# All pairs of four more feed-forwards as halved products, and a fifth ring place that is lent to them

## The reference

```
lat = lat + 0.5 * ml[2] * _swiglu(_modulate(lat, norm_ffn1_g[l], ml[0], ml[1]), *ffn1)
cx  = cx  + 0.5 * mc[2] * _swiglu(_modulate(cx, ...), *ffn1)
h_cx = _modulate(cx, norm_mix_g[l], mc[3], mc[4])
out_cx, s_f, s_b = _token_mixer(h_cx, *mix_w, zero_state, zero_state)    # holds the scan
out_lat, _, _ = _token_mixer(_modulate(lat, ...), *mix_w, s_f, s_b)
lat = lat + 0.5 * ml[8] * _swiglu(_modulate(lat, norm_ffn2_g[l], ...), *ffn2)
def _swiglu(h, w1, w3, w2):  return (jax.nn.silu(h @ w1) * (h @ w3)) @ w2
```

## Time and profile before

| | |
|---|---|
| median of the timed runs | 3034.98 us |
| the profiled execution's own time | 3039.78 us |
| its span, first to last instruction | 3038.0 us |
| PE busy | 2864.5 us, 94% |
| DVE, ACT, POOL busy | 987.1, 550.3, 318.5 us |
| granted PE clock, mean | 0.971 |
| the chain that ended last | PE 85%, DMA 13%, all else 1% or less |

### The profile page before, as it was taken

One profiled execution on the slowest core, in us unless ns is written; L12 is line 12 of the kernel. 1 busy time (PEld: TensorE's weight loads), 2 busy tenths in 40 slices (PEclk: granted clock), 3 DMA queues, 4 the chain that ended last, 5 costly groups with the idle time before them and its releaser, 6 DMA issues.

```text
span 3038.0 us, 38593 instructions
## 1 busy us (share of the span) xinstructions
PE 2864.5 (94%) x16882; PEld 2420.1 (80%) x16882; DVE 987.1 (32%) x1846; ACT 550.3 (18%) x822; POOL 318.5 (10%) x344
## 2 busy tenths in 40 slices
PE   8999999999999999999999999999999999866666
PEld 6888888888888788889888888889988888533432
DVE  3764034331433315333014433523146412210111
ACT  2101222123211101010023206210012340200000
POOL 0000011100121000058001210028100000000000
PEclk9999999999999999999999999999999999988887
DMA  9774443344334566464444344364433228899998
GB/s 402 270 273 171 153 146 133 128 144 153 138 138 131 202 235 230 173 236 166 154 153 153 135 142 153 127 234 168 153 126 136 99 104 339 368 430 430 430 432 361
DMA packets 74139, 641.40 MB, mean 211 GB/s; under 512 B 8304, under 2 KB 9584, under 8 KB 21232
## 3 DMA queue, kind: packets, MB, share of 16 engines
q1 hardware_dynamic: 71376, 631.55, 54.9%
q10 hardware_dynamic: 2592, 7.33, 0.6%
HBM read 637.80 MB, written 1.05 MB: 210 GB/s over the span
## 4 chain that ended last, share of the span: by engine, by line
PE 85%; DMA 13%; DVE 1%; issue 0%; ACT 0%; SPq 0%; DVEq 0%; ACTq 0%
PE ps L1236 34%; PE ps L1258 18%; DMA ring<-in_w_moe 12%; PE ps L1214 8%; PE ps L1433 7%; PE ps L1246 3%; PE ps L1269 3%; PE ps L1463 2%; PE ps L1034 2%; PE ps L1322 1%; DMA ring<-in_w_ada 1%; PE ps L1440 1%; PE ps L1056 1%; PE ps L1161 1%; PE ps L1408 0%; PE ps L1411 0%
## 5 line engine op out<-in xcount | busy, mean ns | idle before, releaser
L1236 PE MATMUL ps<-ring 128*128 128x256 f32 x2560 | 560.7, 380 | 0.1
L1236 PEld LDWEIGHTS ps<-ring 128*128 128x128 f32 x2560 | 485.5, 191 | 67.8 <-issue 1.9
L1258 PE MATMUL ps<-work,ring 128*128 128x256 f32 x2464 | 537.8, 380 | 0.0
L1258 PEld LDWEIGHTS ps<-work,ring 128*128 128x128 f32 x2464 | 466.5, 190 | 64.0 <-issue 2.1
L1236 PE MATMUL ps<-h,ring 128*128 128x256 f32 x2240 | 497.3, 384 | 5.0 <-DVE rs L1898 2.2
L1236 PEld LDWEIGHTS ps<-h,ring 128*128 128x128 f32 x2240 | 429.3, 193 | 68.3 <-issue 6.6
L1895 DVE TENSOR_TENSOR work<-work,ps 128x512 f32<-128x512 f32 (+4 forms) x286 | 133.7, 467 | 631.1 <-PE ps L1236 389.4
L2612 POOL TENSOR_TENSOR work<-work 128x128 f32<-128x128 f32 x168 | 100.1, 632 | 1194.7 <-ACT work L1676 1194.7
L1433 PE MATMUL ps<-h,ring 128*128 128x256 f32 x928 | 205.0, 379 | 0.5 <-DVE h L1901 0.5
L1433 PEld LDWEIGHTS ps<-h,ring 128*128 128x128 f32 x928 | 174.9, 190 | 27.4 <-issue 4.2
L1895 DVE TENSOR_TENSOR work<-work 128x128 f32<-128x128 f32 (+4 forms) x468 | 171.1, 418 | 49.5 <-ACT eb L1678 24.9
(11 more groups left out here) (302 smaller groups left out, 2729.1 us busy)
## 6 DMA issues: line engine op xcount, KB each, us to landing
ring<-in_w SPq DMA_DIRECT2D x182, 1024.0 KB, 4.8
work<-in_w_moe SPq DMA_DIRECT2D x22, 4096.0 KB, 33.4
ring<-in_w_moe SPq DMA_DIRECT2D x22, 4096.0 KB, 33.4
ring<-in_w_in SPq DMA_DIRECT2D x80, 1024.0 KB, 4.8
ring<-in_w SPq DMA_DIRECT2D x56, 896.0 KB, 4.5
work<-in_w_ada SPq DMA_DIRECT2D x40, 1024.0 KB, 6.8
ring<-in_w_ada SPq DMA_DIRECT2D x32, 1024.0 KB, 5.1
ring<-in_w_out SPq DMA_DIRECT2D x16, 1024.0 KB, 4.8
```

Of the source, the lines that this page charges most:

```text
L1236: last = nc.tensor.matmul(ps[:, b, c * L:c * L + L], w[:, k * L + c * P:k * L + c * P + P], hs[cols][:, k, :], start=(k == 0), stop=(k == ...
L1258: last = nc.tensor.matmul(ps[:, b, c * L:c * L + L], w[:, k * L + c * P:k * L + c * P + P], hid[:, k0 + k, :], start=(k0 + k == 0 and c == 0),
```

## The change

- `HALVED` gains four feed-forwards: (0,0,0) pairs 3 to 10, (0,1,1) pairs 2 to 10, (0,0,1) pairs 1 to 10 and (1,1,0) pairs 2 to 10. That is 72 slabs more (16 + 18 + 20 + 18), beside the 38 of before. Three of the four have a scan beside them, (0,0,1) has `vada` stages.
- The ring has five places. The fifth is where the two buffers lie; it is left out of the ring from three slabs ahead of a run's first halved slab to its last (`places`), and POOL waits for its last slab to be done (`lender`).
- A slab's combine stands one slab ahead of it in the list, or two for the first two of a run and behind a gap; `halves` may stand up to four slabs ahead.
- The seven products are taken in another order and to other places in the two banks: PE waits for POOL's sums behind the third product, as before, and no longer for ACT's copy. DVE begins on a halved slab when all of it is done and uses five operations, all of them with one operand in PSUM.

```diff
-RING = 4
+RING = 5
-HALVED = {(1, 0, 0): range(1, 11), (1, 0, 1): range(2, 11)}
-ON_POOL = ((1, 0, 0), (1, 0, 1))
+HALVED = {(0, 0, 0): range(3, 11), (0, 1, 1): range(2, 11), (0, 0, 1): range(1, 11), (1, 0, 0): range(1, 11), (1, 0, 1): range(2, 11), (1, 1, 0): range(2, 11)}
+LENT = 4
...
-        at = max([slabs[mine[0] - 2], ready + 1] + ([busy[-1] + 1] if l == 0 else []))
+        at = max([slabs[mine[0] - 4], ready + 1] + ([read[-1] + 1] if l == 0 and read else []))
         before[at].append(("halves", *run))
-        for i in mine:
-            before[max(slabs[i - 1], at)].append(("combine", *plan[slabs[i]]))
+        for n, i in enumerate(mine):
+            lead = 2 if n < 2 or mine[n - 2] < i - 2 else 1
+            before[max(slabs[i - lead], at)].append(("combine", *plan[slabs[i]]))
...
+def places(slabs):
+    lent = set()
+    for run in HALVED:
+        mine = [k for k, stage in enumerate(slabs) if is_halved(stage) and stage[1:4] == run]
+        lent |= set(range(mine[0] - 3, mine[-1] + 1))
+    last, used = [None] * RING, [0] * RING
+    rows, lender = [], {}
+    for k in range(len(slabs)):
+        free = [i for i in range(RING) if i != LENT or k not in lent]
+        i = min(free, key=lambda i: (-1 if last[i] is None else last[i], i))
...
-                    if k >= RING:
-                        sp.wait_ge(fb_slab, k - RING + 1)
-                    sp.dma_start(ring[:, ring_place(k), 0:width], src).then_inc(w_full[k % RING], 16)
+                    place, after, _ = at.place[k]
+                    if after is not None:
+                        sp.wait_ge(fb_slab, after + 1)
+                    sp.dma_start(ring[:, place, 0:width], src).then_inc(w_full[place - AHEAD], 16)
...
-                        product(bx, 3, b11, a11)
+                        product(bx, 2, b11, a11)
                         product(bx, 0, b21, a12)
                         pe.wait_ge(halves_done, at.halves_at[stage[1:4]] + 1)
-                        product(bx, 2, b22, s4).then_inc(x_mm, 1)
-                        engine, made = at.combined[stage]
-                        pe.wait_ge(combined_p if engine == "p" else combined_d, made)
-                        product(by, 2, b12, s1)
-                        product(by, 1, t3, s3)
-                        product(by, 0, t2, s2).then_inc(y_mm, 1)
-                        pe.wait_ge(one_out, nth + 1)
-                        product(bx, 1, t4, a22).then_inc(fb_slab, 1)
+                        product(bx, 1, b22, s4).then_inc(x_mm, 1)
+                        pe.wait_ge(combined, nth + 1)
+                        product(by, 2, t2, s2)
+                        product(by, 3, t3, s3)
+                        product(by, 1, b12, s1)
+                        product(by, 0, t4, a22).then_inc(fb_slab, 1)
...
                         dve.wait_ge(one_out, at.halved[n] + 1)
-                        dve.wait_ge(y_mm, at.halved[n] + 1)
-                        own(tt(both[:, 0, :], both[:, 1, :], ps[:, by, 0:P], add))
-                        own(tt(both[:, 2, :], both[:, 0, :], ps[:, by, P:2 * P], add))
...
                         dve.wait_ge(fb_slab, at.slab[n] + 1)
+                        own(tt(five[:, 0, :], five[:, 1, :], products(by, 2), add))
+                        tt(five[:, 4, :], five[:, 0, :], products(by, 3), add).then_inc(dve_own, 1)
...
             for stage in plan:
-                if stage[0] == "combine" and on_pool(stage[1:]):
+                if stage[0] == "combine":
...
                     if nth >= 2:
                         pool.wait_ge(fb_slab, at.halved_slab[nth - 2] + 1)
+                    if at.lender[k] is not None:
+                        pool.wait_ge(fb_slab, at.lender[k] + 1)
```

More of the change, by code:

```diff
@@ L217, in with_halves @@
         ready = max(n for n in range(slabs[mine[0]]) if plan[n] == ("norm", l, s, 2 * j))
-        busy = [n for n in range(slabs[mine[0]]) if plan[n][0] == "gmlp"]
-        at = max([slabs[mine[0] - 2], ready + 1] + ([busy[-1] + 1] if l == 0 else []))
+        read = [n for n in range(slabs[mine[0]]) if plan[n][0] == "gmlp"]
+        at = max([slabs[mine[0] - 4], ready + 1] + ([read[-1] + 1] if l == 0 and read else []))
         before[at].append(("halves", *run))
-        for i in mine:
-            before[max(slabs[i - 1], at)].append(("combine", *plan[slabs[i]]))
+        for n, i in enumerate(mine):
+            lead = 2 if n < 2 or mine[n - 2] < i - 2 else 1
+            before[max(slabs[i - lead], at)].append(("combine", *plan[slabs[i]]))
     return [one for more, stage in zip(before, plan) for one in (*more, stage)]
+def places(slabs):
[8 more added lines that the diff above has]
+        i = min(free, key=lambda i: (-1 if last[i] is None else last[i], i))
+        if k in lent:
+            lender[k] = last[LENT] if k - 1 not in lent else lender[k - 1]
+        rows.append((i, last[i], used[i]))
+        used[i] += 1
+        last[i] = k
+        if k in lent and k + 1 not in lent:
+            last[LENT] = k
+    name = {i: AHEAD + n for n, i in enumerate(sorted(range(RING), key=lambda i: last[i]))}
+    return [(name[i], after, n) for i, after, n in rows], lender, name[LENT], {name[i]: last[i] for i in range(RING)}
 def first_order():
@@ L339, in __init__ @@
         self.ada_slab, self.summed, self.out2_at = {}, {}, {}
[L340 to L342 removed]
+        self.halved, self.halved_slab, self.last_halved, self.halves_at, self.sums_at, self.halved_gates = {}, [], {}, {}, {}, set()
+        self.place, self.lender, self.lent, self.last_in = places([stage for stage in plan if is_slab(stage)])
         for n, stage in enumerate(plan):
@@ L2018, in first @@
                         tt(s4, a12, s2, sub).then_inc(halves_done, 1)
[L2019 to L2026, removed]
-                        tt(t3, b12, b22, sub).then_inc(dve_own, 1)
-                        third = S.next(dve_own)
-                        tt(b12, b12, b11, sub)
-                        dve.wait_ge(dve_own, third)
-                        own(tt(t2, b11, t3, sub))
-                        tt(t4, b21, t2, sub).then_inc(combined_d, 1)
@@ L2033, in first, with products @@
                     elif is_halved(stage):
                         which, bx, by = int(kind == "up"), at.group[n] % 4, (at.group[n] + 1) % 4
-                        both, total = part_sums[:, which], sil[:, which, :]
-                        pair = both[:, 0:4, :].rearrange("p (a b) n -> p a b n", b=2)[:, :, 0, :]
+                        five = part_sums[:, which]
+                        c1, c2 = (five[:, 1:5, :].rearrange("p (c t) n -> p c t n", t=2)[:, :, t, :] for t in range(2))
+                        def products(b, place, n=1):
+                            return ps[:, b, place * P:(place + n) * P]
@@ L2044, in first @@
-                        tt(total[:, 0:3 * P], total[:, 0:3 * P], ps[:, bx, 0:3 * P], add).then_inc(ev_d, 1)
+                        own(tt(five[:, 0, :], five[:, 1, :], products(by, 2), add))
+                        tt(five[:, 4, :], five[:, 0, :], products(by, 3), add).then_inc(dve_own, 1)
+                        third = S.next(dve_own)
+                        tt(five[:, 3, :], five[:, 0, :], products(by, 1), add).then_inc(dve_own, 1)
+                        fourth = S.next(dve_own)
+                        dve.wait_ge(dve_own, third)
@@ L2045, in first @@
+                        tt(c2, five[:, 4:5, :].to_broadcast([P, 2, P]), products(by, 0, 2).rearrange("p (c n) -> p c n", c=2), add
+                           ).then_inc(ev_d, 1)
+                        dve.wait_ge(dve_own, fourth)
+                        tt(c1, c1, products(bx, 0, 2).rearrange("p (c n) -> p c n", c=2), add).then_inc(ev_d, 1)
                         if which:
```

57 lines of the change are left out of this document (27 added, 30 removed).

## The result

The changed kernel takes 3135.16 us (median of four runs, 3134.55 to 3136.40) beside 3037.15 us for the kernel before in the same session, 98.0 us more. The ratio of the runs is 1.0336, with a 95% interval of 1.0321 to 1.0351; the two medians alone give 1.0323. Predicted were 3139 us.

What follows compares the result with a forecast made beforehand. PE was taken to bound the stretches beside the scan and `vada`; 72 slabs save 46.7 us, waits add 133.1 and clock 17.6: +104 us on 3039.8, less 4.8 for the timed median, 3139 us, range 3062 to 3172.

Steps and rivals of the forecast that it cites:

- The walk of one head: Beside a scan, from the end of `gate` 6 through `up` 7, DVE and POOL alternating: PE waits 15.9 us a head.
- The turns: DVE decays and POOL combines alternate, one operation each, on shared SBUF interfaces: 15.9 us a head instead of 8.3; chance 0.70.
- the undisturbed walk: The same head with DVE and POOL overlapping as if alone: PE waits 8.3 us; as a rival 3058 to 3076, chance 0.14.
- Waits and clock: Waits of 133.1 us together, plus 2.2 us of lower clock in each of eight heads, 17.6 us.
- The rival that has the clock fall in every gap: Beside the scans each gap's clock drop is paid, two gaps more in seven heads, 31 us more: 3170; chance 0.10.
- The head cycle of 59 us among the signs: Expected in the profile after: a head cycle beside (0,0,0) of about 59 us instead of 47.
- By run: Waits by feed-forward: (0,0,0) 47.4 us, (0,1,1) 36.5, (1,1,0) 39.2, (0,0,1) 10; together 133.1.
- 7.8 without turns: Entry of (1,1,0): third halved slab needs banks at 12.5 us, sums come at 20.3, so PE waits 7.8.
- the 10 of the sum: (0,0,1): `vada` and halved slabs take 93 us on the port against 78 for PE; some 5 slack at either end: 10.
- The fifth place: Between the start and the experts, shorter DMA waits for modulation slabs: taken as 0, between -4 and 0 us.
- The sum: Whole kernel: 133.1 us of waits plus 17.6 of clock less 46.7 of faster slabs, +104 us.

Runs made afterwards that it cites:

- the split operations: The changed kernel with each POOL operation of a combine split into four of 128x128, nothing left out: 3182.97 us, a single execution.
- the quarter combines: The changed kernel with POOL making only the first quarter of each sum, except in each run's first pair: 3057.74 us, ratio 1.0086.
- the places alone: The changed kernel with only the slabs halved that were halved before; five places, new product order and five sums stay: 3024.12 us, ratio 0.9969.
- the fill: The changed kernel with 20 extra PE products, result overwritten, in front of the wait for the combine that follows a `times`: 3130.47 us, ratio 1.0318.

## Why the prediction was right, and where it was not

**The walk of one head** came out nearly as written. E is 487.2, where `gate` 6 ends; in us behind E:

| step | predicted | measured |
|---|---|---|
| first decay ends | 7.9 | 6.9 |
| `gate` 7 starts | 9.7 | 8.5 |
| second decay ends | 14.2 | 12.8 |
| `up` 7 starts | 20.9 | 18.8 |
| `times` ends | 26.0 | 25.0 |
| combine of `up` 7 ends | 31.1 | 30.1 |

The turns are shown by the decays (10.8 us beside a combine, 4.5 alone) and by the split operations; the order by moving the combine, which takes its wait away. Of the undisturbed walk the quarter combines are the trace: `times` starts at E+8.5 there, 8.8 predicted.

**Waits and clock** of a head were split wrongly, and their sum was right. I had 15.9 us of waits a head; the rows show 2.19 + 2.20 + 6.71 = 11.1. I had the clock charged once a head, 2.2 us, because a later wait would hide the rest; the cycle shows 61.28 - (47.24 - 3.9) - 11.1 = 6.8. The rival that has the clock fall in every gap was right of this head in that it fell three times, and wrong in adding the price up. The slow products do not only hide behind the next wait, they shorten it: PE's waits and 3.8 us of slow products (1.9 in `gate` 7, as much ahead of the third gap) fill the 15.9 together, 14.9 measured. Behind the last gap come 2.9 more, 2.2 predicted. Over the three scan runs there are 100 us of waits (123 predicted) and 41 us more, what is left of the 107.7 us of shift and the 33.8 of faster slabs, which I put down to the clock (18 predicted). The head cycle of 59 us among the signs left the clock out; by the prediction's own terms it is 61.4.

**By run**, predicted with its clock and slabs, and measured: (0,0,0) +43.6 and +45.4; (0,1,1) +31.4 and +24.9, where the heads wait twice instead of three times; (1,1,0) +31.9 and +37.4. There the entry waits 15.39 us and 8.21 with quarter combines: 7.8 without turns was about right, and the full combines with their turns add 7.2 and not 4.

**(0,0,1)** was predicted at -3 and costs 3 to 6. One `vada` stage beside the combines takes 8.91 us instead of the 4.99 of the earlier trace rows; the two lines are DVE's stage and three POOL operations beside it:

```profile
1200.58 8.91 DVE L1919 SCALAR_TENSOR_TENSOR work<-work,ring 128x1024 f32<-128x1024 f32 x4
```

```profile
1203.95 6.66 POOL L2604 TENSOR_TENSOR ring<-ring 128x512 f32<-128x512 f32 x3
```

Five gaps follow, 10.7 us, close to the 10 of the sum; their clock was not in it. The 10 itself was loosely worked: 93 less 78 is 15, and with 5 us of slack at both ends 5 would be left.

**The fifth place** is the step that failed: I took 0, between -4 and 0, and the places alone gain 9 (5 to 13). "Behind them PE waits for the norm anyway" holds for 1.27 us of the 2.91 that PE waited at the first spot. The other 1.6 us went, and with them slow products: 1.8 us in the two whole slabs and some 1.2 ahead of them.

**The sum** was +104 with the places at 0; the median moved by 98.0. The mechanism of the heads carries most of that, but that the totals lie so close is in part luck: (0,1,1) came out 6.5 us better and (1,1,0) 5.5 worse than predicted, (0,0,1) 6 to 9 worse, and the places 9 better.

## What to carry to other kernels

Before work is moved to an engine that is idle on average, walk one cycle of the queue it joins: what counts is which instruction stands ahead of it and what that one waits for. Price a wait of a busy TensorE as the wait and, where the clock falls, the slow products behind it, and do not add up waits that slow products fill. A faster form that needs a helper engine is best used only in the places where the helper is free: 70 halved slabs so placed beat 110 by 4%.

## What the runs showed of the hardware

The same length of gap does not always lower the clock. A gap of 2.20 us ahead of `up` 7 is followed by products at half the pace; one of 2.33 us behind the fill, in the same slab, is followed by products at a granted clock of 1.00. Both come behind products at the full clock. Nor does the place decide it: in front of the same whole slab PE waits 2.16 us for DVE before the change (at 1904.25) and with the places alone (at 1894.73); the granted clock behind the wait is 0.50 in the first trace and 1.00 in the second, and the slab takes 8.76 us and 7.17. What tells them apart stays open; no run was made for it.
